# Order of a unit's steps in a hybrid decoder kernel: transposes, value products and the exponential

## The reference

```
prompt, per tile of 128 queries and per head:
  s = q k^T * scale, masked;  p = softmax(s);  o = p v      (selected, window and compressed branch)
  s = q km^T * scale;         p = softmax(s);  o = p vm     (4 memory heads)
sample, per sequence: the same branches over a paged cache of 1024 old tokens
  (the selected blocks come from the cache), a window of 512 and 256 memory tokens
y = rmsnorm(x + concat(o * silu(z)) @ w_out)
```

## Time and profile before

| | |
|---|---|
| median of 3 runs | 934.05 us (933.94 to 935.58) |
| the profiled execution | 935.69 us, span in the trace 933.9 us |
| TensorE busy over the span | 896.8 us (96%) |
| VectorE, ScalarE, GpSimd busy | 520.7, 414.1, 287.4 us |
| mean granted TensorE clock | 0.996 |
| chain that ended last | 83% on TensorE |

### The profile page before, as it was taken

One profiled execution on the slowest core, in us unless ns is written; L12 is line 12 of the kernel. 1 busy time (PEld: TensorE's weight loads), 2 busy tenths in 40 slices (PEclk: granted clock), 3 DMA queues, 4 the chain that ended last, 5 costly groups with the idle time before them and its releaser, 6 DMA issues.

```text
span 933.9 us, 20476 instructions
## 1 busy us (share of the span) xinstructions
PE 896.8 (96%) x7594; PEld 813.0 (87%) x7594; DVE 520.7 (56%) x1501; ACT 414.1 (44%) x1063; POOL 287.4 (31%) x497
## 2 busy tenths in 40 slices
PE   6999999999999999999999999999999999999997
PEld 6999999999999999999988788768877787878885
DVE  4656332422323375565656787676777758745443
ACT  6443221225444201111566666665765667733221
POOL 0123222222225444534144262424322626210000
PEclk9999999999999999999999999999999999999999
DMA  8654413315240544232869058715504142334331
GB/s 229 166 200 147 143 56 141 125 67 122 72 145 28 143 125 120 87 97 68 211 176 242 3 175 275 243 46 140 160 2 132 57 141 75 111 119 147 131 118 67
DMA packets 85220, 117.91 MB, mean 126 GB/s; under 512 B 12930, under 2 KB 67506, under 8 KB 84546
## 3 DMA queue, kind: packets, MB, share of 16 engines
q1 hardware_dynamic: 71666, 73.12, 27.5%
q0 software_dynamic: 10224, 36.20, 11.7%
q10 hardware_dynamic: 3232, 7.28, 2.1%
HBM read 91.50 MB, written 32.02 MB: 132 GB/s over the span
## 4 chain that ended last, share of the span: by engine, by line
PE 83%; DVE 5%; issue 4%; ACT 4%; DMA 2%; POOL 2%; ACTq 0%; DVEq 0%; SPq 0%; POOLq 0%
PE psum L601 9%; PE psum L602 8%; PE psum L603 8%; PE psum L1886 7%; PE psum L1765 5%; PE psum L1742 4%; PE psum L1907 3%; PE psum L1906 3%; PE psum L1905 3%; PE psum L1743 3%; PE psum L852 2%; PE psum L854 2%; PE psum L853 2%; ACT p_P L1995 2%; PE psum L588 2%
## 5 line engine op out<-in xcount | busy, mean ns | idle before, releaser
L601 PE MATMUL psum<-a_whi,f_xhi 128*128 128x256 f32 (+1 forms) x672 | 194.6, 290 | 1.6 <-DVE f_xlo L1077 1.4
L602 PE MATMUL psum<-a_wlo,f_xhi 128*128 128x256 f32 (+1 forms) x672 | 189.9, 283 | 0.0
L603 PE MATMUL psum<-a_whi,f_xlo 128*128 128x256 f32 (+1 forms) x672 | 189.5, 282 | 0.0
L1995 ACT ACTIVATE p_P<-psum,p_nb 128x640 f32<-128x640 f32 (+7 forms) x224 | 124.2, 561 | 45.6 <-DVE p_nb L2067 39.0
L601 PEld LDWEIGHTS psum<-a_whi,f_xhi 128*128 128x128 f32 x672 | 127.0, 189 | 4.0 <-DVE a_wlo L577 1.8
L602 PEld LDWEIGHTS psum<-a_wlo,f_xhi 128*128 128x128 f32 x672 | 127.3, 189 | 0.0
L603 PEld LDWEIGHTS psum<-a_whi,f_xlo 128*128 128x128 f32 x672 | 127.1, 189 | 0.0
L754 POOL DMA_DIRECT2D h_scratch<-a_hst x93 | 50.8, 548 | 232.7 <-DVE a_hst L1137 119.1
L1765 PE MATMUL psum<-f_ident,p_P 128*128 128x128 f32 x656 | 100.1, 277 | 1.6 <-ACT s_KTw L1945 0.7
L1765 PEld LDWEIGHTS psum<-f_ident,p_P 128*128 128x128 f32 x656 | 77.5, 142 | 8.4 <-DVE p_PT L1933 1.8
L2067 DVE CUSTOM_DVE_ANT_0 psum<-psum,p_near 128x256 f32<-128x256 f32 (+7 forms) x96 | 64.6, 673 | 33.7 <-PE psum L1743 28.1
(11 more groups left out here) (339 smaller groups left out, 2166.5 us busy)
## 6 DMA issues: line engine op xcount, KB each, us to landing
a_wraw<-in_w_in SPq DMA_DIRECT2D x24, 512.0 KB, 4.2
h_scratch<-a_hst POOLq DMA_DIRECT2D x72, 128.0 KB, 3.6
s_SG<-in_cache_nsa_slc SPq DMA_DIRECT2D x64, 128.0 KB, 2.3
p_qd<-q_scratch SPq DMA_DIRECT2D x16, 384.0 KB, 7.4
a_xraw<-in_x_prompt SPq DMA_DIRECT2D x8, 512.0 KB, 7.3
s_MK<-in_cache_mem SPq DMA_DIRECT2D x8, 512.0 KB, 8.9
s_WG<-in_cache_nsa_win SPq DMA_DIRECT2D x8, 512.0 KB, 5.0
mix_scratch<-p_zt POOLq DMA_DIRECT2D x8, 512.0 KB, 3.6
```

Of the source, the lines that this page charges most:

```text
L601: nc.tensor.matmul(out, hi, wh, start=first, stop=False)
L602: nc.tensor.matmul(out, hi, wl, start=False, stop=False)
L603: return nc.tensor.matmul(out, lo, wh, start=False, stop=last)
L1995: nc.scalar.activation(dst, s_view(s), ACT.Exp, bias=nb[:, g % NNB:g % NNB + 1], scale=1.0 if s[2] == 3 else -1.0, accum_out=ssum[:, par[i ...
```

## The change

`schedule()` now appends three things in another order within a unit; nothing is computed otherwise and no instruction is added or taken away.

```diff
             partner = mine
+            if v + 2 < NV:
+                steps.append(("sm", v + 2))
+            group = groups.pop(0) if v >= first and groups else []
+            for what, n in group:
+                if what == "t" and n[0] in ("sq", "mk", "mt", "kt", "st"):
+                    add(n)
             while waiting and (l % 2 == 0 or l >= 16) and waiting[0][1] not in mine:
                 pv()
-            if v + 2 < NV:
-                steps.append(("sm", v + 2))
...
-            for what, n in groups.pop(0) if v >= first and groups else []:
-                if what == "t":
+            for what, n in group:
+                if what != "t":
+                    steps.append((what, n))
+                elif n[0] not in ("sq", "mk", "mt", "kt", "st"):
                     add(n)
-                else:
-                    steps.append((what, n))
```

## The result

The changed kernel takes 940.99 us (median of 6 runs, 939.18 to 942.36), the kernel before 934.52 us in the same set (6 runs, 933.27 to 935.63). The ratio is 1.0066, 95% interval 1.0054 to 1.0078: slower by some 6.2 us, where I had forecast no change and a high end of 937.2.

What follows compares the result with a forecast made beforehand. TensorE was taken as the bound, its idle time the most any order could win. Terms -5.1 + 0.55 + 4.9 gave +0.3 us: 936.0 on the profiled execution, 934.4 on the median; range 931.2 to 937.2.

Steps and rivals of the forecast that it cites:

- Part 1: Exponential ahead of the value products: TensorE's waits for exponentials and for copies of sample turns shrink, 5.1 us gained.
- Part 2: `p_OT` copy pushed behind the exponential: value products wait, 0.55 us lost at unit 28, two more places counted as covered.
- Part 3: Sample turns ahead of value products lose the cover for bank waits: 4.9 us lost over ten of 24 units.
- the sum: Gains and losses over the profiled execution: -5.1 + 0.55 + 4.9 = +0.3 us, 935.69 becoming 936.0.
- in the rest the bank is long free: Moved sample turns outside the ten losing units: no loss, or one that falls into a later wait.
- the 0.90 that I booked in unit 56: Unit 56: the key copy that product `sw` needs starts near 610.5 instead of 611.61, so its 0.90 us wait goes.
- the clock as a rival of one fall: One more clock fall, at unit 110, from joined idle time: 1.7 us slower, 936.1 us; chance 0.18.
- its own bounds: Bounds of the range's unknowns: gains from 2.6 to 5.1 us, losses from 1.8 to 6.3, none or one fall.
- halfway between 930.8 and 934.4: Boundary between the faster rival's 930.8 us and the likeliest 934.4 us, given as 932.2.
- I count those two as covered: Waits for `p_OT` of 0.6 us at 627.39 and 0.8 at 720.46, hidden by later vector work; without cover 1.4.
- Rival B: Copies for moved turns come earlier as ScalarE's queue is freed; only losses behind VectorE stay: 930.8 us, chance 0.23.
- Rival D: Half of the exponential's 5.1 us is eaten by VectorE copies while all losses come: 937.7 us, chance 0.15.

Runs made afterwards that it cites:

- the exponential alone: Against the kernel before, only the exponential moved ahead of the value products, sample turns left behind them: 932.24 us, 0.9966.
- halves and filler: Changed kernel with one semaphore per sequence of a pair for page loads, and 22 identity transposes before unit 110's sample turn: 935.84 us, 1.0006.
- the filled variant of the changed kernel: Changed kernel with 22 identity transposes in front of unit 110's sample turn: 939.03 us, 1.0041.
- the halves: Changed kernel with one semaphore per sequence of a pair, so unit 58's turn waits for 8 page loads, not 16: 936.70 us, 1.0010.
- The filler: 22 identity transposes before unit 110's sample turn, added to the kernel with the exponential ahead and only that turn moved: 933.88 us, 0.9987.
- the rule on the banks: Changed kernel with sample turns ahead of value products only in units that have a single own chunk: 932.83 us, 0.9977.
- unit 110 alone: Against the kernel before, exponential ahead everywhere and only unit 110's sample turn moved ahead of its value products: 935.66 us, 1.0008.

## Why the prediction was wrong

**What was right.** Part 1: the four late places won 2.45 us in the profile against 2.41 forecast. The give-backs were larger than I booked (0.35 by unit 119, 0.48 by 115, 0.37 by 55), so the exponential alone is worth 3.2 us, not the 4.6 that part 1 less part 2's 0.55 comes to. Part 2: 0.51 at unit 30 against 0.55. Part 3: the units were right and most sizes near (0.62 / 0.81 / 0.94 against 0.50 / 0.77 / 0.78), with unit 18 and 90 at twice what I took (0.47 and 0.77 against 0.2 and 0.37). The kernel with halves and filler, in which the wait at unit 58 and the idle time of unit 110 are taken away, is at +0.6 us (1.0006, interval -0.4 to +1.4 us), and the sum was +0.3. That the two agree so well is luck: the exponential alone won 3.2 where 4.6 were forecast, and from there to the kernel with halves and filler the turns cost 3.7 (0.9966 to 1.0006) where part 3 had 4.9. The two misses offset each other.

**First failed step: "in the rest the bank is long free".** For unit 58 the bank was free, and the data wasn't there. I had asked of each moved turn only when its PSUM bank came free, and not when its input landed; the trace of before shows no wait, since the pages came some 0.2 us ahead of the turn (614.2, against 614.34). The value product between them (0.37 us, from 613.97 to 614.34) was cover too, and the wins of part 1 moved the turn nearer to a transfer that doesn't move with it, being paced by SyncE from unit 48 on. That took back the 0.90 that I booked in unit 56 and more. Size: 1.5 to 2.3 us of wait, by the execution (1.47 and 2.34 with the same order), with what the clock adds; together with the clock, taking the wait away was worth 5.2 us (the halves).

**Second failed step: the clock as a rival of one fall with a chance of 0.18.** The mechanism was named, its place too, and the size of one fall was near: the changed kernel loses 1.58 us more in units 110 and 111 (2.62 + 0.85) than the kernel whose unit 110 waits as long and had no fall there (1.89); I had said 1.7. The number of falls was wrong. The profiled execution has four against one. One, at 482 us, lies ahead of every moved turn. It is missing in the filled variant of the changed kernel, whose order up to there is the same, and there again in the one with halves and filler: chance. Of the others, those at 618 and 754 us follow the joined waits of units 58 and 110, and the one at 638 us stands where before had its own. No profiled variant has more than two, and the mean clock of this execution is the lowest of its six, so it overstates the number. And the argument against the rival, that the wait of 1.34 at 748.05 before had no fall behind it, compared a wait of half the length. The range, too, was drawn short of its own bounds: the least gain, the largest loss and one fall make 934.05 - 2.6 + 6.3 + 1.7 = 939.4, and the high end was set at 937.2. (A slip beside it: halfway between 930.8 and 934.4 is 932.6, not 932.2.)

**How much each is.** The filler gives a rate: 2.0 us for 0.0025 of mean clock. The changed kernel lacks 0.0044, which makes 3.5 us; if TensorE were the bound in every moment, it would be 0.0044 of 934.5 or 4.1 us. Within the runs of each kernel the slope is smaller, 0.46 us for 0.001, so 2.0 us. There the clock is known to three digits only, and it also counts the end of the kernel, where TensorE has nothing left to do: 1.8 us at half clock in the profile of the rule on the banks, 4.9 us in that of the exponential alone, which is 0.001 and 0.0026 of the mean clock at no cost. A spread of the clock that costs nothing flattens the slope. The traces give a third figure: in the profiled execution the four falls cost some 1.2, 0.65, 1.2 and 1.6 us (against variants that have none in the same units), and the one of before 1.4, so about 3.2 more. So of the 6.2 us I put 2 to 4 to the clock, more likely near the upper end, and the rest of 2 to 4 to waits, of which unit 58 is 1.5 to 2.3. How it divides more finely is open.

**A smaller one: "I count those two as covered".** The `p_OT` waits at units 64 to 66 and 102 weren't covered in the changed kernel: +0.62 and +0.69. I had expected the 0.6 and the 0.8 to vanish behind later vector work. Leaving `p_OT` in front there won 0.61 and 0.29 back, and the second came back as a loss of 0.31 one unit later. So without the moved turns the count was wrong at units 64 to 66 alone, and right at unit 102.

Rival B (copies come earlier by themselves) fell: units 40 and 68 lost what the cover had hidden. Rival D came nearest with its total (937.7, against 941.0), but by a cause that acted only in part: of the 4.6 of part 1 less part 2, the exponential alone kept 3.2.

## What to carry to other kernels

A step that is moved earlier needs two questions, when its output buffer is free and when each of its inputs lands; a transfer that arrives 0.2 us before it is used shows as no wait at all, so read the DMA rows beside the first use, and not the list of waits. An independent product between a wait and the one before it is worth more than its own length: it keeps the idle pieces short. Here a joined wait of 2.6 us was followed by half clock in three of five profiled executions, at 1.6 us each time. Moves that come in one change are best timed apart: here one half was worth -3.2 us and the other +7.6, and the smallest rule that keeps the good half (exponential ahead, `p_OT` first in the first memory unit) is at 0.9957.

## What the runs showed of the hardware that was not expected

- SyncE issues a page load whose address it reads from a table only every 1.1 us (the 16 ahead of unit 58 in 17.26 us, and in 17.2 to 17.8 us over all traces), so 16 of them bound a stage of 19 us even though each lands some 2.2 us after its issue (median of 64, 128 KB each).
- 22 useless transposes made a kernel 2.0 us faster (ratios 1.0008 and 0.9987), with the mean clock going from 0.9952 to 0.9977.
- The clock fell behind the same 2.6 us wait in three profiled executions of five. In one pair it was 0.59 and 1.00 in the stretch behind, with TensorE busy 1.07 and 1.05 us of the 4 us before. That makes a single profile a poor witness of such a cost: the mean clock over the runs told it, the profiled execution of unit 110 alone did not.
